# VectorE's last low parts of a stage wait for GpSimd's folded sum of squares

## The reference, cut to what matters

```python
def rms_norm(x, w):
    xf = x.astype(jnp.float32)
    y = xf * lax.rsqrt(jnp.mean(xf * xf, axis=-1, keepdims=True) + EPS)
    return (y * w.astype(jnp.float32)).astype(x.dtype)
...
    for layer in range(DEPTH):
        h = rms_norm(x, norm_mix[layer])
        x = x + hybrid_mixer(h, w_in[layer], ...)
        h = rms_norm(x, norm_ffn[layer])
        ...
            x = x + swiglu(h, dense_w1[j], dense_w3[j], dense_w2[j])
...
def swiglu(h, w1, w3, w2):
    a = jnp.einsum('bsd,df->bsf', h, w1)
    b = jnp.einsum('bsd,df->bsf', h, w3)
    return jnp.einsum('bsf,fd->bsd', jax.nn.silu(a) * b, w2)
```

## Time and profile before

| | |
|---|---|
| median of 3 runs | 2970.85 us (2970.27 to 2976.11) |
| the profiled execution | 2971.51 us, of which the span is 2969.6 us |
| TensorE matmul busy | 2897.0 us, 98% of the span |
| VectorE busy | 2037.6 us, 69% |
| ScalarE busy | 1627.0 us, 55% |
| GpSimd busy | 330.4 us, 11% |
| mean rate of the DMAs | 207 GB/s |
| mean granted clock of TensorE | 0.991 |

### The profile page before, as it was taken

The page is one execution under the profiler, slowest core; times in us unless marked ns, Lnnn a source line. Parts: engine busy times, 40 slices in busy tenths (PEclk is TensorE's granted clock), DMA queues, the critical chain, the costliest instruction groups (busy, mean ns, idle before and its releaser), DMA issues.

```text
span 2969.6 us, 46613 instructions
## 1 busy us (share of the span) xinstructions
PE 2897.0 (98%) x20144; PEld 2679.1 (90%) x20144; DVE 2037.6 (69%) x1842; ACT 1627.0 (55%) x1603; POOL 330.4 (11%) x224
## 2 busy tenths in 40 slices
PE   8999999999999999999999999999899999999999
PEld 8999999999988888888888787999799999896999
DVE  6787665678768888888888765555555555575553
ACT  6456544545657767767677552445654454362542
POOL 1130310113010000000000002101021111002210
PEclk9999999999999999999999999999999999999999
DMA  7444555544549989989899531556155545540453
GB/s 235 155 142 157 172 185 173 184 145 145 165 181 372 347 346 373 351 335 355 344 370 370 166 128 43 171 177 234 44 170 181 188 150 184 192 142 29 154 180 122
DMA packets 359730, 613.26 MB, mean 207 GB/s; under 512 B 11519, under 2 KB 323925, under 8 KB 324576
## 3 DMA queue, kind: packets, MB, share of 16 engines
q1 hardware_dynamic: 355936, 597.99, 57.8%
q10 hardware_dynamic: 3104, 12.10, 1.2%
q0 software_dynamic: 480, 0.12, 0.0%
HBM read 608.99 MB, written 1.05 MB: 205 GB/s over the span
## 4 chain that ended last, share of the span: by engine, by line
PE 94%; DVE 2%; ACT 2%; POOL 1%; issue 1%; DMA 0%; ACTq 0%; SPq 0%; POOLq 0%; DVEq 0%
PE ps L329 19%; PE ps L330 18%; PE ps L331 18%; PE ps L1269 5%; PE ps L1271 5%; PE ps L1270 5%; PE ps L1245 3%; PE ps L1247 3%; PE ps L1246 3%; PE ps L1810 2%; PE ps L689 2%; PE ps L1825 2%; PE ps L1319 1%; PE ps L1778 1%; PE ps L1766 1%; POOL work L392 1%
## 5 line engine op out<-in xcount | busy, mean ns | idle before, releaser
L273 DVE TENSOR_TENSOR wlo<-raw,whi 128x2048 fp32r<-128x2048 f32 (+2 forms) x574 | 1320.4, 2305 | 445.9 <-ACT whi L262 441.5
L262 ACT ACTIVATE whi<-raw 128x2048 fp32r<-128x2048 f32 (+2 forms) x574 | 1084.5, 1891 | 259.7 <-PE ps L331 134.9
L329 PE MATMUL ps<-HX,whi 128*128 128x256 f32 x1808 | 522.5, 289 | 16.5 <-DVE wlo L273 11.7
L330 PE MATMUL ps<-HX,whi 128*128 128x256 f32 x1808 | 513.9, 284 | 0.0
L331 PE MATMUL ps<-HX,wlo 128*128 128x256 f32 x1808 | 513.8, 284 | 0.0
L329 PE MATMUL ps<-HXB,whi 128*128 128x256 f32 x1760 | 503.0, 286 | 2.7 <-DVE HXB L448 2.7
L330 PE MATMUL ps<-HXB,whi 128*128 128x256 f32 x1760 | 499.7, 284 | 0.0
L331 PE MATMUL ps<-HXB,wlo 128*128 128x256 f32 x1760 | 499.4, 284 | 0.0
L329 PEld LDWEIGHTS ps<-HX,whi 128*128 128x128 f32 x1808 | 349.2, 193 | 22.8 <-ACT HX L524 10.4
L330 PEld LDWEIGHTS ps<-HX,whi 128*128 128x128 f32 x1808 | 349.4, 193 | 3.2 <-issue 3.1
L331 PEld LDWEIGHTS ps<-HX,wlo 128*128 128x128 f32 x1808 | 349.2, 193 | 0.0
(11 more groups left out here) (337 smaller groups left out, 4276.0 us busy)
## 6 DMA issues: line engine op xcount, KB each, us to landing
raw<-in_c_experts SPq DMA_DIRECT2D x264, 1024.0 KB, 4.9
raw<-in_w_in SPq DMA_DIRECT2D x71, 1024.0 KB, 5.0
raw<-in_ff_w_gate SPq DMA_DIRECT2D x44, 1024.0 KB, 5.4
raw<-in_ff_w_up SPq DMA_DIRECT2D x44, 1024.0 KB, 5.3
raw<-in_ff_w_down SPq DMA_DIRECT2D x32, 1024.0 KB, 5.3
raw<-in_dense_w SPq DMA_DIRECT2D x30, 1024.0 KB, 5.3
raw<-in_hy_w_in SPq DMA_DIRECT2D x24, 1024.0 KB, 5.2
raw<-in_ff_w_down SPq DMA_DIRECT2D x16, 768.0 KB, 4.6
```

Source lines behind the costliest of these rows:

```text
L262: e.activation(m.whi[:, i % NSPLIT, 0:n], m.raw[:, i % NRAW, 0:n], ACT.Copy).then_inc(*k.up("act", "hi", i))
L273: e.tensor_tensor(m.wlo[:, i % NRAW, 0:n], m.raw[:, i % NRAW, 0:n], hi, ALU.subtract).then_inc(*k.up("dve", "lo", i))
L329: e.matmul(o, wh, xh, start=first and t == k0, stop=False)
L330: e.matmul(o, wh, xl, start=False, stop=False)
```

## The change

VectorE gets a wait ahead of the last `dve_panel` of a stage: for the event "sq sum" of that stage. It stands in three functions: `dve_out` (called at the ends of hgrn0, hgrn1 and attn), `dve_ffn` (ffn0, ffn1 and ffn2; in ffn3 and ffn4 `nxt` is None) and `dve_hyena` (hy0 and hy1). No other instruction is added, moved or removed.

```diff
@@ -932,6 +932,7 @@
             dve_ahead(e, k, m, s, 2 * j - 2, 2, nxt)
         if j == 3:
             dve_ahead(e, k, m, s, 6, 2, nxt)
+            e.wait_ge(*k.at("sq sum", s))
         dve_panel(e, k, m, panels)
 
 
@@ -1090,6 +1091,8 @@
                 dve_ahead(e, k, m, s, c - 1, 1, nxt)
         if j == 3:
             dve_ahead(e, k, m, s, 7, 1, nxt)
+            if nxt:
+                e.wait_ge(*k.at("sq sum", s))
         dve_panel(e, k, m, panels)
 
 
```

## The result

The changed kernel takes 2949.68 us (median of 4 runs, 2948.06 to 2950.20), against 2973.48 us before (2970.27 to 2976.71, 4 runs). The ratio is 0.9919, with a 95% interval of 0.9902 to 0.9936: 24 us faster. The profiled execution took 2950.17 us, its span is 2948.3 us.

What follows compares the result with a forecast made beforehand. TensorE, busy for 98% of the span, was taken as the bound. Stalls 19.1 us, less 0.1 for held low parts, plus 5.0 for the clock, gave 24.0 us: forecast 2947 us, range 2941 to 2956.

Steps and rivals of the forecast that it cites:

- The fold alone takes 1.3 us: GpSimd's last fold at stage ends, 3.4 to 5.9 us beside line 273, should take about 1.3 us with VectorE held.
- All seven stalls go, 19.1 us: TensorE's idle time of 2.00 to 3.42 us ahead of line 380 at seven stage ends vanishes whole, 19.1 us.
- The held low parts cost 0.1 us: VectorE's low parts (line 273), started later at stage ends, cost 0.1 us in all, at most 0.5.
- the cover: Slack for the held low parts in hgrn0: 5 us before TensorE needs the first; VectorE free 0.4 us before line 462.
- The clock gives 5.0 us in three feed-forward stages: With no idle time before line 380 the clock stays up behind hgrn0, hy0 and attn: 1.56, 1.72 and 1.72 us.
- The stall at the end of ffn0 (hgrn1) 2.0 us: TensorE's idle time ahead of line 380 at the end of ffn0 goes whole, 2.00 us; no clock gain there.
- attn 2.0 without the clock's part: The attention stage gains the 2.00 us stall and no more, as ScalarE's chain from the norm bounds it; clock priced at nothing.
- Pooling 3.4 us: The 3.42 us stall at the end of ffn2 goes; clock priced at nothing, slow matmuls lying beside the norm's Ln and Exp.
- hy1 2.9 us: The stall ahead of line 380 at the end of hy1 goes, 2.92 us; the clock already stayed up there.
- hgrn1's own wait is worth 0: At the end of hgrn1 the fold is done before line 273 starts, so the wait is already met: 0 us.
- What would show it: Signs: folds about 1.3 us, no idle time before line 380, clock 1.00 behind it, TensorE idle 19 us and busy 5 to 8 lower.
- The rival in which the clock's gain moves elsewhere: Stalls go, but falls of the clock come at other places: 2952 us, or 2955 with two new falls; chance 0.2.

Runs made afterwards that it cites:

- wait_behind_one: Changed kernel with the wait moved behind the first low part, so line 273 runs once against the last fold; 2956.47 us.
- fill_wait: Kernel before, no new wait; TensorE multiplies ones by ones 8 to 14 times while waiting ahead of line 380 at seven stage ends; 2970.48 us.
- again: The changed kernel measured and profiled once more, nothing altered; 2948.27 us, ratio 0.9913 to the kernel before.
- Fill_pool: Changed kernel plus nine matmuls of ones by ones in TensorE's idle time in pooling; 2949.36 us.
- own_pair: Kernel before, no new wait; GpSimd leaves out the last fold at seven stage ends and TensorE adds up the last two chunks itself; 2953.42 us.
- part_out: Kernel before plus only the wait in dve_out (ends of hgrn0, attn and hgrn1); 2967.15 us, ratio 0.9980.
- part_ffn: Kernel before plus only the wait in dve_ffn (ends of ffn0, ffn1 and ffn2); 2968.50 us, ratio 0.9983.
- early_fill: Changed kernel with the pooling windows' DMA issued in the middle of ffn2 and nine matmuls of ones by ones in pooling; 2948.60 us.

## Why the prediction was right

2947 us was forecast with a range of 2941 to 2956; 2949.68 was measured, and 2948.27 in the second round. By ratios, 24.0 us were forecast, and 24 and 26 measured.

- **The fold alone takes 1.3 us**, from the one quiet fold in pooling: right, 1.29 to 1.31, and 1.52 at hy0 and hy1 where it meets VectorE's last scaled low part. wait_behind_one shows the cause: low parts shut it out, one by one. The spacing of starts and the reported spans agreed here.
- **All seven stalls go, 19.1 us**: right. Two of the seven carried VectorE's name in the trace, and went with the others.
- **The held low parts cost 0.1 us**: right in what it cost, but not in the cover. I had VectorE free 0.4 us ahead of line 462 in hgrn0. I had taken 3.54 us from line 380 to line 462, from a stretch with the low clock; at 1.00 the factor comes sooner. It was there at 341.25 (the end of line 373), but line 462 began at 341.61, behind the low parts, where before it had begun 0.10 behind the factor. So the reader came 0.26 us late, and in pooling 0.33. In hgrn0 TensorE had other work meanwhile, and ffn0 did not get longer.
- **The clock gives 5.0 us in three feed-forward stages**: right, and some 0.1 high each. Fill_wait measured 1.48, 1.58 and 1.59, together 4.65. Over the whole execution 5.1 us less were lost to the clock in "again", but only 1.7 less in the profile of the first round, with a fall near its start and 1.7 us more lost in moe to hy0. In the change the same stretches gave stall and clock as forecast: 4.57 for 4.47, 4.69 for 4.64, 4.69 for 4.65.
- **The stall at the end of ffn0 (hgrn1) 2.0 us**: right, 2.24.
- **attn 2.0 without the clock's part**: the size is right, 1.91. The reason given, that the chain from the norm bounds the stage, was not what decided: the clock's part was not won at all, since the fall came later in the same stage. 8.5 us were lost to the clock there before and after. Fill_wait, with 1.7 less lost, gained 0.46, so little of it lies on the path, as forecast.
- **Pooling 3.4 us**: the mis-sized term; it measured 2.09. That the slow matmuls lie beside the norm's Ln and Exp was right: from line 380 to line 477 it took 3.01 us before and 2.94 after. What failed was to price the clock at nothing or a gain. With the stall gone, TensorE is through with its input products sooner and idle while the norm is made, and the clock fell behind that, on the 32 matmuls with the windows, which are on the path (8.86 us for 7.14). Fill_pool won 1.5 us back. But idle time alone does not settle it: in own_pair the same 0.92 and 1.22 us were followed by no fall.
- **hy1 2.9 us**: right, 3.17. That the clock had stayed up behind the 2.92 us of idle time there before is no property of the place: in part_out and part_ffn it fell behind the same stall.
- **hgrn1's own wait is worth 0**: right as far as can be told. VectorE's first low part behind it began with no idle time that GpSimd ended; the stretch from moe to hy0, which scatters by 3.5 us, can't show it.
- **What would show it**: TensorE's busy time was to be lower by 5 to 8 us and its idle time by 19. They were lower by 4.0 and 17.3, and in "again" by 5.8 and 17.8. Part of the idle time came back as the 0.92 us ahead of line 477.
- The rival in which the clock's gain moves elsewhere was partly true, of part_out and part_ffn most, but of the whole too: new falls in pooling and at the start of ffn3, one fewer in hy1. That they nearly cancel, and that the sum came out at 23.4 of 24.0 with pooling 1.3 short, is in part luck.

## What to carry to other kernels

When GpSimd makes a small result on which TensorE waits, look for the same instruction somewhere with VectorE idle: the difference is what work with two inputs in SBUF on VectorE does to it, and a wait on VectorE that has slack can be the cheapest cure. Price a stall of TensorE with the lower clock behind it, about 1.5 us here, but only in a stretch that TensorE bounds, and as something that may come or not: behind the same stalls in hgrn0 and hy1 the clock fell in some kernels and not in others. And compare stretches between two fixed events rather than totals: where an edit acted and no fall of the clock differed, they repeated within some 0.1 us, while the total of one kernel scattered by 2 to 10. A total divided by the number of places can mislead, as in own_pair.

## What the runs showed of the hardware

The blocking goes both ways: at the end of ffn0 two low parts together took 5.59 us before and 4.49 after, so VectorE's was held by GpSimd's fold as well, and line 394 by the second low part. Here are VectorE and GpSimd there in the kernel before, and VectorE at the end of ffn1, which repeats the pattern and shows the two low parts apart:

```profile
529.44 5.59 DVE L273 TENSOR_TENSOR wlo<-raw,whi 128x2048 fp32r<-128x2048 f32 x2
```

```profile
532.95 2.66 POOL L394 TENSOR_TENSOR work<-work 128x256 f32<-128x256 f32 x1
```

```profile
2053.10 2.29 DVE L273 TENSOR_TENSOR wlo<-raw,whi 128x2048 fp32r<-128x2048 f32 x1
2055.63 3.05 DVE L273 TENSOR_TENSOR wlo<-raw,whi 128x2048 fp32r<-128x2048 f32 x1 [0.25 <-ACT whi L262]
```

In ffn1 VectorE had to wait 0.25 us for ScalarE between its two low parts, and the fold got in there (3.43 us in all). In hgrn0 the second low part followed at once, and the fold had to wait for both (5.49). The Trainium skill (SBUF — State Buffer, section Who interferes with whom) says that whichever instruction begins first has the shared ports for its whole length; both the 1.15 us behind the end of a low part and these rows agree with it. The granted clock fell behind idle times of 2.00 us (ffn1) and 2.91 (hgrn0), and did not behind others of 2.00 (ffn0) and 2.92 (hy1). With the same idle time at hy1 it fell in two other kernels, and in hgrn0 it did not in one (part_ffn). The Trainium skill (TensorE: Matmul & The Clock Gate, Part 1) calls the windows of activity free-running, with which this agrees. The stretch from moe to hy0 differs by 3.5 us between kernels whose work there is the same (1013.62 in wait_behind_one, 1017.10 in early_fill). It goes with the clock in the main: where 6.8 us were lost to it, as before and in "again", the stretch took 1013.6 to 1014.5 us; where 8.5, 1014.5 to 1017.1; and where 10.2 (part_ffn, fill_wait), 1016.5 and 1016.6. The rest, 2.6 us among kernels that lost 8.5, stays open.
